# Query means of a hybrid encoder layer: nine matmuls in a row, or three at a time between rows of the pooling tiles

## What is computed

```python
xn = rms_norm(h, attn_norm_g[l])
proj = xn @ w_in[l]
q, k, v, u = jnp.split(proj, splits, axis=-1)        # 512, 128, 128, 512 columns
q = apply_rope(rms_norm(q, q_norm_g[l]), cos, sin) * q_scale
k = apply_rope(rms_norm(k, k_norm_g[l]), cos, sin)
attn = sliding_sink_attention(q, k, v, sinks[l])     # 8 query heads of 64, 2 key heads, chunks of 64
pool = multiscale_pool(u, w_pool[l], pool_scale[l])  # trailing means over 2, 4, 8, 16 positions
h = h + jnp.concatenate([attn, pool], axis=-1) @ w_out[l]
```

## Time and profile before

| what | us |
|---|---|
| median of three runs | 1064.39 |
| lowest and highest run | 1061.08, 1064.53 |
| profiled execution, device time | 1060.28 |
| profiled execution, span from first to last instruction | 1057.7 |
| TensorE busy | 1037.7 (98%) |
| VectorE, ScalarE, GpSimd busy | 686.5 (65%), 464.1 (44%), 104.1 (10%) |
| mean granted clock of TensorE | 0.995 |

### The profile page before, as it was taken

One profiled execution on the slowest core, in us unless ns is written; L12 is line 12 of the kernel. 1 busy time (PEld: TensorE's weight loads), 2 busy tenths in 40 slices (PEclk: granted clock), 3 DMA queues, 4 the chain that ended last, 5 costly groups with the idle time before them and its releaser, 6 DMA issues.

```text
span 1057.7 us, 18708 instructions
## 1 busy us (share of the span) xinstructions
PE 1037.7 (98%) x7880; PEld 991.9 (94%) x7880; DVE 686.5 (65%) x1018; ACT 464.1 (44%) x706; POOL 104.1 (10%) x108
## 2 busy tenths in 40 slices
PE   7999999999999999999999999999999999999998
PEld 7988999999999999999999989999989999899987
DVE  6678644569945599455546794556697566975452
ACT  6886534434423343223348773453343233432322
POOL 1253000110001100010003510000000000000000
PEclk9999999999999999999999899999999999999999
DMA  7211232222333222322231203223223332233212
GB/s 235 81 50 41 90 111 81 81 82 79 106 100 115 81 81 80 120 81 90 93 98 41 90 2 120 80 84 116 80 73 120 90 117 81 71 122 90 98 60 79
DMA packets 94106, 94.94 MB, mean 90 GB/s; under 512 B 3424, under 2 KB 92856, under 8 KB 94024
## 3 DMA queue, kind: packets, MB, share of 16 engines
q1 hardware_dynamic: 93456, 93.58, 27.7%
q10 hardware_dynamic: 312, 0.18, 0.1%
q0 software_dynamic: 256, 0.01, 0.0%
HBM read 91.65 MB, written 2.10 MB: 89 GB/s over the span
## 4 chain that ended last, share of the span: by engine, by line
PE 84%; DVE 8%; ACT 5%; issue 2%; DMA 1%; POOL 0%; SPq 0%; DVEq 0%; ACTq 0%; POOLq 0%
PE slot L567 65%; PE slot L951 12%; PE slot L769 2%; ACT rot_s L1221 2%; PE slot L801 1%; PE slot L616 1%; PE slot L1011 1%; PE slot L829 1%; PE slot L836 1%; DVE ms_work L1607 1%; DVE h L1912 1%; DMA x_in<-in_x 1%; PE slot L818 0%; DVE m_op_lo L1876 0%; ACT w_hi L409 0%
## 5 line engine op out<-in xcount | busy, mean ns | idle before, releaser
L567 PE MATMUL slot<-x_hi,w_hi 128*128 128x264 f32 (+2 forms) x1516 | 354.9, 301 | 3.4 <-DVE w_lo L420 3.0
L567 PE MATMUL slot<-x_lo,w_hi 128*128 128x264 f32 (+2 forms) x1516 | 351.5, 299 | 0.0
L567 PE MATMUL slot<-x_hi,w_lo 128*128 128x264 f32 (+2 forms) x1516 | 351.1, 298 | 0.0
L567 PEld LDWEIGHTS slot<-x_hi,w_hi 128*128 128x128 f32 x1516 | 247.3, 190 | 15.0 <-issue 3.9
L567 PEld LDWEIGHTS slot<-x_hi,w_lo 128*128 128x128 f32 x1516 | 245.9, 190 | 7.5
L567 PEld LDWEIGHTS slot<-x_lo,w_hi 128*128 128x128 f32 x1516 | 246.0, 190 | 7.3
L420 DVE TENSOR_TENSOR w_lo<-raw,w_hi 128x2048 fp32r<-128x2048 f32 (+2 forms) x68 | 154.3, 2270 | 91.6 <-ACT w_hi L409 91.6
L409 ACT ACTIVATE w_hi<-raw 128x2048 fp32r<-128x2048 f32 (+2 forms) x68 | 123.9, 1822 | 150.8 <-PE slot L567 95.8
L1115 POOL TENSOR_TENSOR work<-work 128x528 f32<-128x528 f32 (+1 forms) x32 | 41.9, 1308 | 707.1 <-DVE work L1836 348.6
L1394 ACT ACTIVATE work<-gate,par_all 128x528 f32<-128x528 f32 (+1 forms) x44 | 31.9, 731 | 134.8 <-DVE gate L1563 67.8
L951 PE MATMUL slot<-m_op_hi,w_hi 128*128 128x264 f32 (+1 forms) x256 | 73.7, 288 | 1.3 <-DVE h L1912 0.8
(11 more groups left out here) (209 smaller groups left out, 1663.2 us busy)
## 6 DMA issues: line engine op xcount, KB each, us to landing
raw<-in_w_gate SPq DMA_DIRECT2D x44, 512.0 KB, 4.8
raw<-in_w_up SPq DMA_DIRECT2D x44, 512.0 KB, 4.4
raw<-in_w_down SPq DMA_DIRECT2D x32, 512.0 KB, 4.5
raw<-in_w_in SPq DMA_DIRECT2D x19, 512.0 KB, 4.9
raw<-in_w_out SPq DMA_DIRECT2D x16, 512.0 KB, 4.0
raw<-in_w_down SPq DMA_DIRECT2D x16, 384.0 KB, 3.8
x_in<-in_x SPq DMA_DIRECT2D x4, 512.0 KB, 6.9
out<-y_out SPq DMA_DIRECT2D x4, 256.0 KB, 2.3
```

What stands on the lines that cost most here:

```text
L567: ins = nc.tensor.matmul(out_part, w[ws][:, r, cols], a[:, k, tokens], start=first and n == 0 and w is w_hi and a is a_hi, stop=end and w ...
```

## The change

`q_means` gets a range of blocks. The wait for the squares and the opening of the output area stay with the first block, the increment with the last. `q_means(0)` is cut into three groups of three matmuls that stand behind the first, second and third row of u3; `q_means(1)` into three groups between fill rows. The order of rows of u3 and of fill rows among themselves moves a little: fill rows 0 and 1 come behind row 6 of u3 instead of row 5. All other orders on all engines stay.

```diff
-                def q_means(kv):
+                def q_means(kv, b0, b1):
 
-                    s = open_slot(f"qn{kv}", l)
-                    pe.wait_ge(headsq_ready, l * 5 + (2 * kv + 3))
-                    for b in range(NB):
+                    s = ps.slot(f"qn{kv}")
+                    if b0 == 0:
+                        open_slot(f"qn{kv}", l)
+                        pe.wait_ge(headsq_ready, l * 5 + (2 * kv + 3))
+                    for b in range(b0, b1):
                         ins = nc.tensor.matmul(slot[s][:, 0, 2 * b:2 * b + 2], head_sq[:, b, :],
                                                cst[:, C_BLK:C_BLK + P:HEAD_DIM], start=True, stop=True)
-                    ins.then_inc(filled[s], 1)
+                    if b1 == NB:
+                        ins.then_inc(filled[s], 1)
...
-                q_means(0)
-                u3_rows(0, 6)
+                u3_rows(0, 1)
+                q_means(0, 0, 3)
+                u3_rows(1, 2)
+                q_means(0, 3, 6)
+                u3_rows(2, 3)
+                q_means(0, 6, 9)
+                u3_rows(3, 7)
                 fill(0, 2)
-                u3_rows(6, 7)
-                fill(2, 3)
                 u3_rows(7, 8)
-                fill(3, 6)
-                q_means(1)
+                fill(2, 4)
+                q_means(1, 0, 3)
+                fill(4, 5)
+                q_means(1, 3, 6)
+                fill(5, 6)
+                q_means(1, 6, 9)
                 scores(0)
                 fill(6, 8)
                 scores(1)
```

## The result

The changed kernel takes 1073.78 us (median of 6 runs, 1070.58 to 1074.35). The kernel before, timed beside it, takes 1060.49 (6 runs, 1058.91 to 1064.53). The ratio is 1.0112, with a 95% interval of 1.0091 to 1.0132: 1.1% slower, some 12 us (the medians lie 13.3 us apart). The forecast was 1074.0. The profiled execution took 1070.58 us, its span is 1068.6 against 1057.7: +10.9 us, where the sum said +11.4. It is the fastest of the six; the other five took 2.9 to 3.8 us more, and no trace shows where.

What follows compares the result with a forecast made beforehand. TensorE, 98% busy, bounds the kernel. Late scores (9.5 us) plus clock (1.9) make +11.4: 1071.7 from the profiled 1060.28, 1075.8 from the median 1064.39; the forecast went between, 1074, range 1068 to 1080.

Steps and rivals of the forecast that it cites:

- the sum: Whole kernel: 9.5 us from late first scores plus 1.9 us for the clock, +11.4 us; as leading case, chance 0.62.
- The bound: TensorE, busy 98% of the span: a microsecond its queue loses is the kernel's unless a wait swallows it.
- a, the wait in front of u3: TensorE before u3: idle 3.2 us instead of 1.2, small matmuls after it, 2.06 us a layer; crossings free.
- b, when the means are ready: ScalarE's squares of query tile 2 wait for qn0: start 4.8 us later in layer 0, 4.7 in layer 1.
- c, the chain from the squares to the first scores: ScalarE and GpSimd, 10.7 us without slack: whole delay reaches the scores, TensorE idles nearly 3 us; 9.5 us both layers.
- d, qn1 in pieces: Second query means in three pieces between fill rows: same work, priced at nothing, covered by TensorE's idle time.
- e, the clock behind the first scores: Half-clock dip behind the first scores in both layers, after 3 us idling: 1.5 us in layer 0, 0.4 in layer 1.
- Rival 2: Clock stays low through the mixed stretch behind the restart and longer behind the scores: 5 us more, 1079; chance 0.17.
- Rival 4: Mixing keeps the clock up, removing three dips: 4.1 us back against 4.1 us of moved work, 1064.4, no change; chance 0.07.

Runs made afterwards that it cites:

- e6: Changed kernel plus 24 useless dense matmuls in the wait ahead of u3 and a second buffer for the squares of tiles 2 and 3; 1063.53 us, ratio 1.0006.
- e1: Changed kernel with qn0's nine matmuls again in one run ahead of u3 row 0, qn1 still in three groups; 1060.84 us, ratio 1.0007.
- e5: Changed kernel plus 24 useless dense matmuls in the wait ahead of the first u3 row; 1069.99 us, ratio 1.0079.
- e2: Changed kernel with qn0's nine matmuls in one run behind the third row of u3; 1072.53 us, ratio 1.0122.
- e4: Changed kernel with a second buffer for the squares of tiles 2 and 3, so ScalarE need not wait for qn0; 1071.56 us, ratio 1.0106.
- e7: Changed kernel with qn0's three groups moved between the last rows of q3, ahead of the wait, plus 9 useless dense matmuls in it; 1062.13 us, ratio 1.0007.
- e8: As e7, plus four fill rows (6 to 9) ahead of the first scores and rows 10 to 13 moved up; 1058.74 us, ratio 0.9977.
- e9: Changed kernel with a second squares buffer, qn0's nine in one run behind all of u3 and four fill rows, its root behind tile 3's shift; 1069.15 us, ratio 1.0078.
- e10: As e8, without the 9 useless dense matmuls in the wait; 1059.49 us, ratio 0.9992.

## Why the prediction was right

The total, the sign and most terms held, and one step was wrong without showing in the total. That the forecast of 1074.0 met 1073.78 so closely is in part luck: it stood on a base of 1064.39, which six runs put at 1060.49, and took 1.8 us off its own sum. As a difference it promised 9.6 us over its base, the sum 11.4, and 12 to 13 were measured.

- **The bound** (TensorE; its lost time is the kernel's): right. The 10.9 us of the span are found to 0.1 in TensorE's timeline.
- **a, the wait in front of u3**: right, 3.07 us for 3.2. As a cost of its own it is nearly gone where both causes are taken away (0.2 us a layer in e6's profile). Crossings cost nothing, as taken: those of qn1 in e1, and those of qn0 in e5, where three rows and three groups take 61.59 - 57.40 = 4.19 us at full clock, no more than 3 x 0.73 + 2.06.
- **b, when the means are ready**: 4.8 and 4.7 us later were forecast, it was 6.39 - 1.26 = 5.13 and 5.09. The value of 0.22 us for a small matmul at half clock, chosen between bounds, measures 0.213 (e2). When the clock falls and comes back was wrong twice, and the two nearly cancel: it fell 1.97 us behind the restart instead of 1.03, which brought row 2 on 0.98 us earlier than in my sum, and it had not come back for row 2 and the third group, which cost 1.29. The Trainium skill ("TensorE: Matmul & The Clock Gate", section "LDWEIGHTS (loading the stationary operand)") gives a load's time as its columns over 1.2 GHz, with no term for the array's clock; for 128 columns that is an estimate of 0.107 us. At full clock the step of 0.115 us here is near it, but at half clock it became 0.213, so the rule does not hold for these float32 loads.
- **c, the chain from the squares to the first scores**: the 10.7 us from the start of the squares to the scores were carried over unchanged (74.45 - 63.78 = 10.67). **The step that failed** is "TensorE itself gets there earlier ... at about 71.7. It then stands idle for nearly 3 us". It arrived at 74.2 and waited 0.24 us. The idling that I had named was used up: the half clock lasted 10.24 us, not 3.4. That the sum did not suffer is luck: the late chain and the slow engine ended at the same time. e4 shows what the mistake would have cost: by my working it had to gain about 3 us a layer (13.9 us to the scores instead of 17.06), and it gained none (18.33 and 16.83).
- **d, qn1 in pieces**: nothing, right (e1).
- **e, the clock behind the first scores**: in both layers, right, but not for the reason given: the 3 us of idling that were to lie ahead of it were 0.24 and 0.21, and 3.4 us at half clock came all the same. The net cost is 1.06 in layer 0 (I took 1.5) and 0 in layer 1 (0.4): a dip of 3.4 us at this place costs 1.06, the same number as between the layers of before.
- **Rival 2** (the clock stays low in the mixed stretch) was right as a mechanism and wrong in price. Its 1.2 us a layer for row 2 and the third group came (1.29), but the later fall gave 0.98 of them back, and the longer stretch at half clock behind the scores (1.3 us a layer) did not come: it was 3.4 us there. So it added 0.3 us a layer, not 2.5. The Trainium skill ("TensorE: Matmul & The Clock Gate", section "Loop structure matters more than you think") has it that dense sequences keep the engine warm and waits between them cool it. The trace agrees in sign, with 10.24 us behind the longer wait; but the section names waits, whereas TensorE had no gap in those 10 us.
- **Rival 4** (the clock pays for the moved work) needs both conditions of e6, and is then near, in the profiled execution: 0.2 us a layer. Its reason is wrong: the mixing does not keep the clock up, without the matmuls in the wait it prolongs the half clock.

## What to carry to other kernels

In a queue worked in order, ask of small work what it hides in before spreading it: here nine means lay inside a wait, and one dense row put in front of them took them out and made an engine two steps further late. When two things arrive at the same moment, taking either away gains little; test them in a square of four runs. If small matmuls are to be mixed with dense ones, ahead of the wait was harmless here (e7, 1.0007) and behind it cost 1.1%; that mixing them there gains anything is not shown, since e8 also moves fill rows. Look at the granted clock for several microseconds after, even where the engine never waits.

## What the runs showed of the hardware

- A 2-column float32 matmul with its 128 x 128 load takes 0.115 us at 2.4 GHz and 0.213 at 1.2 GHz (18 records in 2.06 and in 3.83 us).
- TensorE stayed at 1.2 GHz for 10.24 us while it was busy all the time, in a stretch that mixes small and dense matmuls behind a wait of 3.1 us (13.66 in e4); purely dense work behind a wait of 1.2 us was at 1.2 GHz for 3.4 us (before, e1). After the same 3.1 us of wait, dense work saw 3.4 us of it in one layer and none in the other (e9). Once low, it stayed low through 6 us of dense rows behind the last small matmul (changed kernel).
- The same mixed stretch was at 2.4 GHz throughout when 24 dense matmuls filled the wait (e5 and e6, both layers of the one profiled execution of each).
- The clock also fell with no wait ahead of it: behind small matmuls between fill rows, after 10.1 us in which TensorE had no gap, it was low for some 10 us (e8 in layer 0, e10 in layer 1).
